# Attention's half of the output projection, made inside the recurrence's TensorE program, in a PSUM bank of its own

## What is computed

```python
mix = jnp.concatenate([sb_out, rw_out], axis=-1)   # attention: 512 channels, RWKV-7 recurrence: 512 channels
x = x + mix @ w_out[l]                             # the output projection
h2 = rms_norm(x, norm2_gain[l])
x = x + hierarchical_moe(h2, ...)                  # routing, then 32 experts
```

## Time and profile before

| | us |
|---|---|
| median of 3 runs | 2705.53 (2703.35 to 2707.84) |
| the profiled execution, its own time | 2712.85 |
| its span, first to last instruction | 2711.1 |
| recurrence at full swing: 11 turns, 1173.5 to 1504.3 | 330.8 |
| routing stage: 11 tiles in steady state, 1694.5 to 1879.8 | 185.3 |
| experts, from 1928.4 | 782.7 |

### The profile page before, as it was taken

The page is one execution under the profiler, slowest core; times in us unless marked ns, Lnnn a source line. Parts: engine busy times, 40 slices in busy tenths (PEclk is TensorE's granted clock), DMA queues, the critical chain, the costliest instruction groups (busy, mean ns, idle before and its releaser), DMA issues. The chain is left out here.

```text
span 2711.1 us, 87599 instructions
## 1 busy us (share of the span) xinstructions
PE 2541.3 (94%) x37008; PEld 1572.4 (58%) x37009; DVE 1174.1 (43%) x2439; ACT 1058.0 (39%) x2119; POOL 773.3 (29%) x916
## 2 busy tenths in 40 slices
PE   7999999999999999688888888999799999999998
PEld 3444444444467777477777754555455566555564
DVE  2333321111299999466666632334422222222222
ACT  1111110000177778566666533444133333333333
POOL 0000030000000000466666611112344444444443
PEclk9999999999999999899999999999799999999999
DMA  4111131111122203011111106553399988889993
GB/s 145 59 58 58 58 113 62 48 68 46 56 79 76 76 10 110 26 45 48 41 48 46 44 12 193 186 186 117 116 314 326 324 297 290 304 296 373 303 320 84
DMA packets 227325, 370.01 MB, mean 136 GB/s; under 512 B 35009, under 2 KB 116417, under 8 KB 224418
## 3 DMA queue, kind: packets, MB, share of 16 engines
q1 hardware_dynamic: 213186, 328.72, 35.1%
q0 software_dynamic: 13920, 38.03, 5.9%
HBM read 296.17 MB, written 70.52 MB: 135 GB/s over the span
## 5 line engine op out<-in xcount | busy, mean ns | idle before, releaser
L2341 PE MATMUL gu_ps<-gate_up_,xT 128*32 128x256 f32 x6336 | 362.0, 379 | 9.0 <-issue 6.9
L347 PE MATMUL ps<-low,high 128*128 128x512 f32 x768 | 337.7, 596 | 2.4 <-issue 2.4
L2412 DVE STREAM_TRANSPOSE xT<-xg 128x256 f32<-128x256 f32 x145 | 95.2, 656 | 483.6 <-PE gu_ps L2341 480.0
L2341 PEld LDWEIGHTS gu_ps<-gate_up_,xT 128*32 128x32 f32 x6336 | 205.5, 110 | 151.6 <-DVE h L2426 29.7
L2390 ACT COPY y<-y_ps 32x256 f32<-32x256 f32 x576 | 210.1, 365 | 193.6 <-PE y_ps L2350 179.3
L2350 PE MATMUL y_ps<-down_,hT 128*32 128x256 f32 x4608 | 276.8, 379 | 1.7 <-ACT y L2390 1.7
L347 PEld LDWEIGHTS ps<-low,high 128*128 128x128 f32 x768 | 144.6, 192 | 173.5 <-issue 173.5
L722 DVE TENSOR_TENSOR_SCAN h_all<-h_all 128x512 f32<-128x512 f32 x192 | 243.0, 1325 | 3.3 <-ACT h_all L680 2.9
L1782 PE MATMUL ps<-high 128*128 128x512 f32 x512 | 232.1, 604 | 8.8 <-DMA high<-mixT 8.8
L2309 POOL DMA_INDIRECT out<-y,put x144 | 194.6, 1351 | 158.8 <-ACT y L2390 92.1
L2301 POOL DMA_INDIRECT xg<-h,take x146 | 144.8, 992 | 293.9 <-DVE h L2426 235.8
(11 more groups left out here) (325 smaller groups left out, 4331.3 us busy)
## 6 DMA issues: line engine op xcount, KB each, us to landing
down_<-in_w_exp_down SPq DMA_DIRECT2D x128, 512.0 KB
gate_up_<-in_w_exp_gate SPq DMA_DIRECT2D x88, 512.0 KB
gate_up_<-in_w_exp_up SPq DMA_DIRECT2D x88, 512.0 KB
high<-in_w_exp_gate SPq DMA_DIRECT2D x40, 512.0 KB
high<-in_w_exp_up SPq DMA_DIRECT2D x40, 512.0 KB
pT<-low SPq DMA_DIRECT2D x13, 1024.0 KB, 3.9
rkv<-pT SPq DMA_DIRECT2D x96, 128.0 KB, 2.6
high<-in_x SPq DMA_DIRECT2D x16, 512.0 KB, 3.9
```

The lines of the kernel that those rows point to most:

```text
L347: done = pe.matmul(qkv_ps[:, part, :], hT[:, s, k, :], w_sb[:, k, part * SBW:(part + 1) * SBW], start=(k == 0), stop=(k == KT - 1))
L2341: last = pe.matmul(gu_ps[QUARTERS[q], 0:2 * P].rearrange("t (x f) -> t x f", x=2), xT[:, k * ROWS:(k + 1) * ROWS], w_gu[s][:, k, :, q * P: ...
L2412: dve.transpose(xT[:, :].rearrange("p (k t) -> p k t", k=KT), xg[j][:, :].rearrange("t (p k) -> t k p", k=KT))
```

## The change

Attention's four blocks of the product are made, for tiles 2 to 15, in turns 0 to 13 of the recurrence: tile 2+n in turn n, 8 products a turn, with the sum kept in a PSUM bank of its own (`half_ps`, bank 7). The residual's x is loaded by halves, DVE adds the bank to it, SP stores it to the output tensor; the routing stage loads that in place of x, and makes four products a half where it made eight. PE's helper counts its own instructions (`place`): in each stretch of 256 the first call that ends at or behind 176 is followed by one product. The count begins at 172 and adds 17 a turn for waits. What is left over is made before `output_and_state(b, 2)` and at the end of the turn; by this count 103 of the 112 products stand at such places and 9 are left-overs. R keeps one bank, so the uses of its two banks now take turns, with the waits that this needs: the low-rank products are split in `lora_decay` and `lora_rate`, and ACT's `decay` moves ahead of `key_squares` and `copy_T(n, 3)`.

```diff
-        X, Y, Z, R = [ps[:, 2 * x:2 * x + 2, :] for x in range(4)]
+        X, Y, Z = [ps[:, 2 * x:2 * x + 2, :] for x in range(3)]
+        R, half_ps = ps[:, 6, :], ps[:, 7, :]
+        PAGE, NEAR_END, PLACE, WAITS_A_STEP = 256, 176, 172, 17
...
             def _(sp):
+                def store_half(n, half):
+                    sp.wait_ge(mix.half_added, 2 * n + half + 1)
+                    mix.store_part(sp, early(n), half)
+
+                def load_half(n, half):
+                    if n >= 1:
+                        sp.wait_ge(mix.part_stored[half], n * 16)
+                    mix.load_x(sp, early(n), half)
...
                 for n in range(-1, STEPS + 2):
+                    if 1 <= n <= N_EARLY:
+                        store_half(n - 1, 1)
+                        if n + 1 < N_EARLY:
+                            mix.load_early(sp, early(n + 1))
+                        if n < N_EARLY:
+                            load_half(n, 0)
                     if there(n + 3):
                         load_lora(n + 3)
...
+                    if 0 <= n < N_EARLY:
+                        load_half(n, 1)
+                        store_half(n, 0)
...
             def _(act):
...
                     if there(m + 1):
+                        decay(m + 1)
                         key_squares(m + 1)
                     if there(n):
                         copy_T(n, 3)
                     if there(m + 1):
-                        decay(m + 1)
                         rate(m + 1)
...
             def _(dve):
+                def add_half(n, half):
+                    dve.wait_ge(mix.part_loaded[half], n * 16 + 16)
+                    dve.wait_ge(mix.half_done, 2 * n + half + 1)
+                    dve.tensor_tensor(mix.part[:, half, :], mix.part[:, half, :], half_ps, ALU.add).then_inc(mix.half_added, 1)
...
                         grow_X1(n, 0)
+                    if 0 <= n < N_EARLY:
+                        add_half(n, 0)
                     if there(b):
                         state(b, 2)
...
                         largest_root(m + 1)
+                    if 0 <= n < N_EARLY:
+                        add_half(n, 1)
...
             def _(pe):
                 def mm(out, lhsT, rhs, start=True, stop=True):
-                    return pe.matmul(out, lhsT, rhs, start=start, stop=stop)
+                    nonlocal place, page
+                    done = pe.matmul(out, lhsT, rhs, start=start, stop=stop)
+                    place += 4
+                    if turn is not None and place // PAGE != page and place % PAGE >= NEAR_END:
+                        page = place // PAGE
+                        early_product()
+                    return done
+
+                def early_product():
+                    nonlocal place, made
+                    if made == 2 * mix.EARLY:
+                        return
+                    half, k = made // mix.EARLY, made % mix.EARLY
+                    if made == 0:
+                        pe.wait_ge(mix.weights, 16 * KT)
+                        pe.wait_ge(mix.rows_loaded[early(turn) % 2], turn // 2 * 16 + 16)
+                    if k == 0:
+                        pe.wait_ge(mix.half_added, 2 * turn + half)
+                    done = pe.matmul(half_ps, mix.rows[:, early(turn) % 2, k, :], mix.w[:, k, half * 512:(half + 1) * 512], start=(k == 0), stop=(k == mix.EARLY - 1))
...
-                def lora_products(m):
+                def lora_decay(m, n, t):
                     pe.wait_ge(tanh_ready, m + 1)
+                    if there(t):
+                        pe.wait_ge(out_ready, t + 1)
...
+                def lora_rate(m):
+                    pe.wait_ge(sig_ready, m + 1)
+                    lora_product(m, 1).then_inc(lora_done, 1)
...
                 def key_norm(m):
                     pe.wait_ge(sq_ready, m + 1)
-                    pe.wait_ge(sig_ready, m + 1)
+                    pe.wait_ge(a_ready, m + 1)
...
+                def gate(t, n):
+                    pe.wait_ge(gate_ready, t + 1)
+                    if there(n):
+                        pe.wait_ge(bonus_ready, n + 1)
...
                         level_X1(n, 0)
+                    if turn is not None:
+                        finish_half(0)
                     if there(b):
                         output_and_state(b, 2)
...
                         level_T(n, 2)
                     if there(m + 1):
-                        lora_products(m + 1)
+                        lora_decay(m + 1, n, t)
...
                         level_T(n, 3)
+                    if there(m + 1):
+                        lora_rate(m + 1)
...
                         level_X1(n, 4)
+                    if turn is not None:
+                        finish_half(1)
+                    if there(n):
                         from_state(n, 0)
...
     def load_rows(self, sp, t, s):
-        sp.dma_start(self.rows[:, s, :, :], self.dram[:, :, bass.ds(t * P, P)]).then_inc(self.loaded[s], 16)
+        sp.dma_start(self.rows[:, s, :, :], self.dram[:, self.EARLY:KT, bass.ds(t * P, P)]).then_inc(self.rows_loaded[s], 16)
...
+    def rest_products(self, pe, s, half):
+        for k in range(self.EARLY, KT):
...
                 def load(t, s):
-                    sp.dma_start(x_t[:, s, :], x[0, bass.ds(t * P, P), :]).then_inc(x_loaded[s], 16)
+                    rows = x[0, bass.ds(t * P, P), :] if isinstance(t, int) and t < mix.WHOLE else x1_dram[bass.ds(t * P, P), :]
+                    sp.dma_start(x_t[:, s, :], rows).then_inc(x_loaded[s], 16)
...
-                sp.wait_ge(mixed, 1)
-                mix.load_rows(sp, 2, 0)
...
-                sp.wait_ge(mixed, 2)
-                mix.load_rows(sp, 3, 1)
```

More of the change, by code:

```diff
@@ L975, in vec, with early, whole_rows @@
             return vecs[:, v, pair(m, st):pair(m, st) + 1]
+        N_EARLY = NT - mix.WHOLE
+        def early(n):
+            return mix.WHOLE + n
+        def whole_rows(t):
+            slot = (STEPS - 3 + t) % 3
+            return rkv[:, slot, :, :, :].rearrange("p a s t -> p (a s t)")[:, 0:KT * P].rearrange("p (k t) -> p k t", t=P)
         def wide(mask):
@@ L1088, in decay @@
                 def decay(m):
-                    act.wait_ge(lora_done, m + 1)
+                    act.wait_ge(lora_done, 2 * m + 1)
                     if m >= 1:
@@ L1184, in log_variance @@
                     act.wait_ge(var_done, t + 1)
-                    act.activation(both(rstd), R[:, 1, :], ACT.Ln, bias=zero_eps[:, 1:2], scale=1.0 / HD).then_inc(lnvar_ready, 1)
+                    act.activation(both(rstd), R[:, :], ACT.Ln, bias=zero_eps[:, 1:2], scale=1.0 / HD).then_inc(lnvar_ready, 1)
                 act.wait_ge(consts, 1)
@@ L1389, in _, with finish_half @@
                 TILES = [(st, HS[h], HS[h] if st == 0 else HS[1 - h]) for h in range(2) for st in range(2)]
+                place = PLACE
+                turn, made, page = None, 0, -1
                 def mm(out, lhsT, rhs, start=True, stop=True):
-                    return pe.matmul(out, lhsT, rhs, start=start, stop=stop)
+                    nonlocal place, page
[16 more added lines that the diff above has]
+                    done = pe.matmul(half_ps, mix.rows[:, early(turn) % 2, k, :], mix.w[:, k, half * 512:(half + 1) * 512], start=(k == 0), stop=(k == mix.EARLY - 1))
+                    if k == mix.EARLY - 1:
+                        done.then_inc(mix.half_done, 1)
+                    place += 4
+                    made += 1
+                def finish_half(half):
+                    while made < (half + 1) * mix.EARLY:
+                        early_product()
                 def every(one):
@@ L1614, in mix_rows @@
                     if part == 0:
-                        pe.wait_ge(mix.weights, 16 * KT)
+                        pe.wait_ge(mix.weights, 16 * KT + 16 * mix.WHOLE)
                         pe.wait_ge(X1_ready, STEPS * NL)
-                    if part % 8 == 0:
-                        pe.wait_ge(mix.loaded[s], 16)
-                    mix.products(pe, s, half, (k, k + 1))
+                        pe.wait_ge(mix.half_added, 2 * N_EARLY)
+                    mix.whole_products(pe, whole_rows(s), s, half, (k, k + 1))
                 pe.wait_ge(consts, 1)
@@ L1625, in _ @@
                     m, b, t = n + 1, n - 1, n - 2
+                    if 0 <= n:
+                        place += WAITS_A_STEP
+                    turn, made = (n if 0 <= n < N_EARLY else None), 0
                     if there(n):
@@ L1661, in _ @@
                     if there(t):
-                        gate(t, m)
+                        gate(t, n)
                     if n == STEPS + 1:
@@ L1966, in mix_half @@
                     if half == 0:
-                        pe.wait_ge(mix.loaded[s], n * 16 + 16)
+                        pe.wait_ge(mix.rows_loaded[s], (mix.early_each + n) * 16)
                         pe.wait_ge(x1_ready, CREDIT + t - 1)
-                    mix.products(pe, s, half, range(KT))
```

(3 more changed lines are left out.)

113 lines of the change are left out of this document (68 added, 45 removed).

## The result

The changed kernel takes 2757.11 us (median, 2750.57 to 2758.88), the kernel before 2706.69, measured with it (2703.35 to 2707.89): a ratio of 1.0189, interval 1.0175 to 1.0203. It is **slower by 50 us**, where the prediction had 17 us less. The profiled execution has a span of 2757.1 against 2711.1.

The account below looks back on a forecast made before the run. PE was taken to bound the kernel nearly everywhere. Recurrence and ends add 43 us, routing saves 60: -17, from the median of 2705.5 to 2688.5 us; own range 2681 to 2706, 8-in-10 range 2655 to 2720.

Parts of the forecast that it names:

- the pauses: Recurrence: PE idles 3.7 us a turn awaiting the next 256 instructions; this is the room for moved products.
- Term 1: Recurrence: eight moved products of 0.86 us, 6.9 a turn, mostly covered by idle time; 2.0 us a turn uncovered.
- Term 2: Recurrence: the moved products' own instructions, 32 and some waits a turn, cost 0.5 us a turn.
- Term 3: Recurrence: DVE's two adds from PSUM, the second delaying the masks, cost 0.3 us a turn (bounds 0 and 0.7).
- Term 4: Recurrence: R in one bank puts ACT's decay earlier and makes PE wait for the sigmoid, 0.2 us a turn (0 to 1.5).
- SP's transfers in the recurrence: Recurrence: SP's new 256 KB loads and stores and their waits cost nothing.
- Routing: Routing stage: tiles fall from 16.85 to 10.9 us, late rows lose 2.4 a pair; 60 us saved (45 to 72).
- The first: Rival, recurrence: pauses are not room or products miss them; 7.9 us a turn added, 2756 us; chance 0.17.
- Full cover: Rival, recurrence: all product time is covered, leaving 18 us of other terms; 2663 us; chance 0.20.
- The sigmoid: Rival, recurrence: PE is held by ACT's sigmoid, 2.1 us in 16 turns; 31 us more, 2719; chance 0.07.
- The fourth rival: Routing stage stops at another limit, late rows or x: tiles of 13 us, 2718 at worst, 2705 milder; chance 0.09.
- The rule: Skill page against the forecast: instruction fetch overlaps execution, crossings are "mostly hidden", so no pause would exist to fill.

Follow-up runs that it names:

- a_w512_twice: a_w512 with a second extra product near the middle of each stretch of 256 instructions, up to 16 a turn: 2926.98 us, turns of 44.92.
- a_split: The kernel before with R in one bank alone, no products, adds or transfers added: 2720.56 us against 2704.68, turns of 30.22.
- a_quads: a_w512 with each extra product made as four 64x64 pieces, two at a time side by side: 2843.00 us, turns of 39.21.
- after: The changed kernel itself, as profiled, against the kernel before: 2757.11 us (ratio 1.0189), turns of 36.7 us.
- a_w512: a_split plus 8 full-width (512 columns) products a turn at the change's places, result unused, no waits, adds or transfers: 2786.90 us, turns of 35.15.
- rows first: The changed kernel with SP issuing the rows of even tiles ahead of the expert weights instead of behind them: 2731.44 us.

## Why the prediction was wrong, step by step

**What bounds the kernel, and the pauses: right but for the picture.** The count of places was right: 84 packets. The cover was right in size: the forecast had 6.9 - 2.0 = 4.9 us a turn, the runs give 4.8 at the price that `a_w512_twice` shows. Part of that is luck. The picture was of a pause at each end that a product drops into; but products in the middle or far from the ends are covered nearly as well, so that picture isn't needed, and products of 16 columns lengthened the stretch by 11 us with 18.5 still idle, so idle time isn't filled before time is added. The part that held is the argument by period: 3.99 us for 256 instructions, of which PE is busy for 3.41 (283.4 / 83). At full width the products used 33.6 of `a_split`'s 37.6 us of idle time.

**Term 1, the products: this is the step that failed.** It priced a product at 0.86 us, from weight loads 0.43 apart in the routing stage, where it stands among its like. Between 64x64 tiles it costs 1.22. Eight times 0.36 are 2.9 us a turn, 40 us in 14. That 0.34 of it come with the change of tile is shown in three ways: the hole is 0.47 us with 16 columns in it, and 0.09 in a quarter of the array; these products add 30.2 us to PE's busy time in eleven turns, 0.34 each, nearly all of it (26.3 us) with the step from a quarter of the array to the whole; and cut into 64x64 pieces (`a_quads`) a product takes 1.72 us, its columns' time alone. What the engine does in the 0.15 us in front and the 0.10 that each matmul takes longer, the traces don't show.

**Term 2, the instructions:** 0.5 forecast, 0.2 measured. Terms 1 and 2 together: 2.5 forecast, 4.93 measured.

**Term 3, DVE's adds: the wrong side was priced.** On DVE they cost nothing, not even 0.3. But the first product of a half waits until the half before it is out of the bank, and the add at the turn's end is queued on DVE behind `grow_X1(n, 4)` and `largest_root`. Here are these three (L1324, L1366, L1371) and the product that waits:

```profile
1377.66 0.69 DVE L1324 TENSOR_TENSOR XX<-XX,ps 128x512 f32<-128x512 f32 x1 [1.34 <-PE ps L1444]
1378.26 0.68 DVE L1366 TENSOR_SCALAR sq<-ps 128x512 f32<-128x512 f32 x1
1378.87 0.68 DVE L1371 TENSOR_TENSOR high<-high,ps 128x512 f32<-128x512 f32 x1
```
```profile
1379.69 1.10 PE L1463 MATMUL ps<-high 128*128 128x512 f32 x2 [1.00 <-DVE high L1371]
```

It makes 10.9 us of idle time on PE in 11 turns, 1.0 a turn, and 1.2 by the runs (36.67 - 35.15 - 0.28). The forecast listed SP's new waits and who stands behind them, and left out this one, on the engine that bounds the stage. The turn of `after` is 1.5 longer than that of `a_w512`; this wait is most of it.

**Term 4, R in one bank:** 0.14 a turn against 0.2, both within the spread, right where it was looked at. It was costed in turns at full swing alone; `a_split` shows 16 us over the whole run. The "1 for the two others" should have been some 10 for the fill and drain of the pipeline.

**SP's transfers in the recurrence:** nothing forecast; 0.28 a turn at most, adds included.

**Routing: right but for a size.** 54.1 us saved against 60, with short and long tiles in turn. The short ones are 10.9 to 11.2 us, as forecast (10.9). The long ones are 15.8 to 16.7: the rows cost 5.3 us a pair where 2.4 was forecast. PE waits 4.5 us for them, 0.8 more than reckoned, and a term is missing: with that rest the granted clock goes to 0.50 for some 7 us, and the next eight products take 6.3 us instead of 3.68, 2.6 more. Of these 7.1 us, 1.8 are absorbed, so there was slack (1.3 in the forecast). With rows first the stage saves 76.7 us.

**The sum.** A full turn: 4.93 + 1.5 + 0.14 = 6.6 us against 3.0 forecast. Turns 0 to 13 give 95.8 us more (17.4 + 72.5 + 5.9) against 42; routing saves 6 less; start, end and turns 14 and 15 add 10.4 against 1. That is 53.8 + 5.9 + 9.4 = 69.1, less 6.1 of "all else": 63, from the forecast -17 to +46.

**The rivals.** The first gave 2756 and has the number, 2757, and its sign, turns of 36 us or more, but not for its reason, so the agreement is chance: the products neither miss the ends nor go uncovered. Its 7.9 a turn would be nearly 11 had nothing been covered at the true price. Half of the sentence that would turn the sign was right: 3.3 us uncovered was the point, and 4.9 came. Full cover didn't occur. The sigmoid doesn't hold PE in the changed kernel (1.5 us in 11 turns); with R's change alone it does (11.4), hidden again by products. The fourth rival occurs in its milder form, and added to the loss.

**The rule.** The Trainium skill (page "Runtime: NRT & Kernel Launch", section on instruction fetch mechanics) calls such a crossing "mostly hidden". The trace of before spoke against it, with 3.7 us a turn idle, and the runs hold to that: with `a_w512_twice` nothing is idle, and without products there is room of 4.8. In the changed kernel, with PE busy for 4.59 us in each 256, it is hidden, as the page says.

**Where the gain went.** A moved product gives back 54.1 / 112 = 0.48 us in the routing stage, 0.69 with rows first. It costs 0.62 in the recurrence by itself and 0.81 with its waits ((36.67 - 30.22) / 8). With rows first it is nearly a draw before the fixed costs of the shared bank. At 0.49 us, fewer products (every second end) with rows first would be on the right side by 0.2 each, about 10 us for some 50 products if each gave back as much, against 16 for the bank; that wasn't run. No version that was run beats the kernel before.

## What to carry to other kernels

Price a moved operation by what it costs among its new neighbours, not where it stands now: a product over the whole array amid 64x64 tiles took 1.2 us instead of 0.86. Idle time in the records is at best an upper bound for what can be hidden; put in a dummy of a few columns first, and double the real one, to see what is covered and what an uncovered one costs. Look at the granted clock wherever a change makes TensorE wait. When work gets a PSUM bank of its own, ask both who waits for that bank on the engine that bounds the stage, and what the others lose where the pipeline fills and drains.

## What was not expected of the hardware

- Full-array products that compute almost nothing (16 columns) lengthen the time by 0.13 us each, while PE's idle time halves; in a quarter of the array they cost 0.02 each.
- The cover isn't bound to the place: products in the middle of a stretch cost 0.05 us each more than at its end, which is at the spread, those placed by calls 0.09.
- Once PE is busy for 4.6 us in 256 instructions, its idle time on issue is 1.7 us in 403; with 30.1 us turns it was 40.7 in 331.
- Amid 64x64 tiles a product over the whole array costs 1.20 us, 0.34 more than its columns; cut into 64x64 pieces, two at a time, it costs 1.72, its columns alone.
- With a wait of TensorE of 4.6 us in the routing stage come 6.8 us at a granted clock of 0.50, in which the next eight products take 2.6 us more.
